# Stick-breaking projections as 512-column blocks that are turned on VectorE and fetched back from device memory

## The chip, the core and the metric
One core of one Trainium2 chip runs the whole program in one launch. The metric is the device time of that launch in microseconds, the median of several runs; here 1634.8 us (three runs, 1633.47 to 1635.04). The rows below come from one profiled execution, which took 1634.64 us and has a span of 1632.9 us from its first to its last instruction.

## The reference
Two decoder layers over 256 tokens with 2048 features, each with a residual sub-layer and a cross-attention sub-layer, and one final RMSNorm. The change lies in the sub-layer of the second (odd) layer, which is stick-breaking attention with 16 heads of 128 features:

```python
u = h @ w_in_odd[o]                     # (256, 2048) @ (2048, 8192)
q, k, v, gate = jnp.split(u, 4, axis=-1)
z = einsum('bhtd,bhsd->bhts', qb, kb) * scale
log_keep = where(mask, log_sigmoid(-z), 0)
rev = cumsum(log_keep[..., ::-1])[..., ::-1] - log_keep
A = where(mask, exp(log_sigmoid(z) + rev), 0)
att = A @ v
x = x + (att * silu(gate)) @ w_out_odd[o]
```

Everything else (pooling mixer and HGRN2 in the first layer, a cross-attention with four heads after each) is unchanged in what it computes.

## The kernel before
All large products run in full precision by splitting each float32 operand into a high part (fp32r) and a low part: a product is hi*hi + hi*lo + lo*hi. The weights come as units of 256 output columns, 136 of them (names `C_KV0` to `C_END` number them), each in four pieces of 512 KB. For every piece, SyncE loads it into `raw`, ScalarE writes its high part into `wpair` (`split_hi`, line 684), VectorE its low part (`split_lo`, line 985), and TensorE multiplies. `wpair` holds exactly one unit, so the split of a piece can begin only when TensorE has done the same piece of the unit before, and has to be finished when TensorE comes round again, three pieces later.

TensorE, ScalarE and VectorE each have an order written out by hand. `slot(c, steps)` is what ScalarE or VectorE does while TensorE is in unit c: for p in 0 to 3, split piece p of unit c+1, then the steps listed at p. A step marked `END` stands ahead of the split at p = 3 and waits for the end of unit c. On TensorE, a hook `(p, work)` runs behind piece p. All engines work strictly in this order, so a step that waits holds up all splits behind it.

There are two forms of product. `chunk(..., "T")` (lines 345, 348) keeps the weights still and moves the tokens: one unit, 256 features on the partitions by 256 tokens, per k-tile two matmuls of 512 columns and two of 256. `block` (line 393) keeps the tokens still and moves 512 weight columns: two units at once, tokens on the partitions, per k-tile six matmuls of 512 columns. What comes out of a block stands the other way round. Where features are needed on the partitions, `turn_block` transposes 32 by 32 squares on VectorE, SyncE stores the 512 KB into a small tensor in device memory (`key_store`, line 243) and fetches them back with the squares in their places, in four DMAs (line 248). The two residual stages and the cross-attention keys already do this.

The stick-breaking stage (`C_SB`, units 80 to 111) goes pair by pair of heads, i = 0 to 7. Values of eight heads at a time come as two blocks; queries, keys and gate of each pair are three chunks. For a pair, TensorE computes the logits z (`sb_logits`, lines 634, 636), ScalarE and VectorE make softplus (900 to 906, 1443, 1447), VectorE its reversed running sum (1456, 1461), ScalarE the exponential (913), VectorE masks it (1469, `sb_weights`); then TensorE turns the weights (`turn`, line 645), ScalarE copies them (926), TensorE multiplies them with the values (`mix_values`, 653, 655), and `sb_outputs` (1484 to 1489) applies the gate. Turning and mixing of pair i are hooks in the first unit of pair i+1; the last pair's are hooks of the output stage `out_stage(C_OUT1)`.

In an `out_stage` the residual is brought up to date unit by unit, and GpSimd scales and squares each unit (lines 1569, 1553, 1555), while ScalarE (711) and VectorE (1181) split the scaled unit into high and low parts. In the stage `C_OX0`, VectorE also splits the features of the memory (`mem1_lo`, line 1020) for the stage behind it, `C_KV1`.

## Time and profile before

| what | value |
|---|---|
| median of three runs | 1634.8 us |
| the profiled execution | 1634.64 us, span 1632.9 us |
| TensorE busy | 1622.3 us, 99% of the span |
| VectorE busy | 1139.3 us, 70% |
| ScalarE busy | 792.3 us, 49% |
| GpSimd busy | 150.7 us, 9% |
| stick-breaking stage | 949.7 to 1330.3 us of the span |

The busy time of TensorE says that it nearly always has a matmul in flight, and not how fast it goes: neighbouring matmuls overlap, so the distance between their starts is what a unit costs. VectorE and ScalarE have time to spare on average, but within one pair of heads their steps form a chain that TensorE waits for at its end.

### The profile page before, as it was taken

The numbers are of one execution on the slowest core, as the hardware profiler recorded it, in microseconds if no ns is written. First come the engines' busy times: TensorE is split into PE (matmuls) and PEld (weight loads), VectorE is DVE, ScalarE is ACT, GpSimd is POOL, SyncE is SP. The second block draws the span as 40 slices with busy tenths as digits, with TensorE's granted clock in tenths as the row PEclk, the third lists the DMA queues.
The fourth block names the chain that finished last, engine by engine and source line by source line (L and its number), as shares of the span: only waits on it lengthen the run. The fifth ranks groups of instructions, "written<-read, shape, count | busy, mean of one in ns | idle before, by whom it ended". The sixth has DMA issues, their size and how long they took to land.

```text
span 1632.9 us, 22719 instructions
## 1 busy us (share of the span) xinstructions
PE 1622.3 (99%) x8842; PEld 1393.6 (85%) x8842; DVE 1139.3 (70%) x1273; ACT 792.3 (49%) x957; POOL 150.7 (9%) x103
## 2 busy tenths in 40 slices
...
GB/s 283 243 250 195 217 193 168 168 181 156 167 179 203 221 170 141 154 202 241 224 242 226 193 192 185 179 168 168 185 177 162 187 175 220 198 168 160 149 188 135
DMA packets 243236, 310.61 MB, mean 190 GB/s; under 512 B 10192, under 2 KB 181584, under 8 KB 243024
## 3 DMA queue, kind: packets, MB, share of 16 engines
...
## 4 chain that ended last, share of the span: by engine, by line
PE 96%; DVE 1%; DMA 1%; ACT 1%; SPq 0%; issue 0%; ACTq 0%
PE ps L345 35%; PE ps L393 32%; PE ps L348 17%; PE ps L410 5%; PE ps L489 1%; PE ps L469 1%; DMA raw<-xa_wkv 1%; PE ps L645 0%; PE ps L636 0%; PE ps L653 0%; PE ps L549 0%; DVE wpair L985 0%; SPq L283 0%; PE ps L572 0%; PE ps L480 0%; DVE ypair L1020 0%
## 5 line engine op out<-in xcount | busy, mean ns | idle before, releaser
L985 DVE TENSOR_TENSOR wpair<-raw,wpair 128x1024 fp32r<-128x1024 f32 x536 | 692.0, 1300 | 377.0 <-ACT wpair L684 375.1
L684 ACT ACTIVATE wpair<-raw 128x1024 fp32r<-128x1024 f32 x536 | 567.7, 1060 | 731.0 <-PE ps L348 389.5
L345 PE MATMUL ps<-xpair,wpair 128*128 128x512 f32 x1920 | 608.3, 398 | 0.0
L393 PE MATMUL ps<-wpair,ypair 128*128 128x512 f32 x1920 | 440.1, 391 | 1.9 <-DVE ypair L1020 1.9
L348 PEld LDWEIGHTS ps<-xpair,wpair 128*128 128x128 f32 x1920 | 360.7, 188 | 85.1
L393 PEld LDWEIGHTS ps<-wpair,ypair 128*128 128x128 f32 x1920 | 360.6, 188 | 76.9 <-issue 2.2
L348 PE MATMUL ps<-xpair,wpair 128*128 128x256 f32 x1920 | 377.5, 278 | 0.0
L345 PEld LDWEIGHTS ps<-xpair,wpair 128*128 128x128 f32 x1920 | 293.7, 189 | 2.0 <-issue 0.6
L345 PE MATMUL ps<-ypair,wpair 128*128 128x512 f32 x448 | 140.9, 396 | 0.0
L1569 POOL TENSOR_TENSOR scratch<-xT,par 128x512 f32<-128x512 f32 x24 | 29.4, 1223 | 824.2 <-issue 771.6
L348 PEld LDWEIGHTS ps<-ypair,wpair 128*128 128x128 f32 x448 | 84.2, 188 | 19.9
L1004 DVE TENSOR_REDUCE tmp<-ps 128x512 f32<-128x1024 f32 x66 | 80.6, 1220 | 21.8 <-PE ps L348 21.7
L410 PE MATMUL ps<-wpair,ypair 128*128 128x512 f32 x384 | 88.5, 390 | 0.0
L348 PE MATMUL ps<-ypair,wpair 128*128 128x256 f32 x448 | 88.0, 278 | 0.0
L393 PE MATMUL ps<-wpair,xpair 128*128 128x512 f32 x384 | 87.9, 390 | 0.0
L393 PEld LDWEIGHTS ps<-wpair,xpair 128*128 128x128 f32 x384 | 71.9, 188 | 14.8
L410 PEld LDWEIGHTS ps<-wpair,ypair 128*128 128x128 f32 x384 | 71.6, 188 | 14.7
L345 PEld LDWEIGHTS ps<-ypair,wpair 128*128 128x128 f32 x448 | 68.4, 189 | 0.4 <-DVE tmp L1230 0.2
L1555 POOL TENSOR_TENSOR acc<-acc,sq 128x512 f32<-128x512 f32 x24 | 42.1, 1755 | 1.9
L345 PE MATMUL ps<-wpair,xpair 128*128 128x512 f32 x128 | 40.5, 397 | 0.0
L1553 POOL TENSOR_TENSOR sq<-xT 128x512 f32<-128x512 f32 x24 | 38.9, 1619 | 0.0
L348 PEld LDWEIGHTS ps<-wpair,xpair 128*128 128x128 f32 x128 | 24.0, 188 | 5.7
...
## 6 DMA issues: line engine op xcount, KB each, us to landing
raw<-w_in_odd SPq DMA_DIRECT2D x128, 512.0 KB, 3.9
...
```

The costliest lines, as they stand in the source:

```text
L345: mm(ps[:, 2 * parity + j, :], still[:, k, 0, j * P:(j + 1) * P], move[:, k].rearrange("p h n -> p (h n)"), start=(k == 0), stop=False)
L348: last = mm(ps[:, 2 * parity + j, S:2 * S], still[:, k, 1, j * P:(j + 1) * P], move[:, k, 0], start=False, stop=(k == KT - 1))
L393: last = mm(ps[:, 2 * parity + r, :].rearrange("p (b n) -> p b n", b=2), operand[:, k, x_part, r * P:(r + 1) * P], wpair[:, KP * p + 2 * a ...
L410: last = mm(ps[:, 2 * (e % 2) + r, :].rearrange("p (b n) -> p b n", b=2), ypair[:, k, x_part, r * P:(r + 1) * P], wpair[:, KP * p + 2 * a: ...
L469: last = mm(ps[:, 4, r * S:(r + 1) * S].rearrange("p (m a t) -> p m a t", m=2, a=4), xq_qp[:, k, q_part, r * P:(r + 1) * P], in_rows(ypair ...
L489: last = mm(ps[:, 6 + b // 2, (b % 2) * S:(b % 2 + 1) * S], xq_v[:, m, v_part, b * P:(b + 1) * P], xq_pt[:, m, p_part, :], start=(m == 0 a ...
L684: fn(wpair[:, KP * p:KP * (p + 1), 0, :], raw[:, p], ACT.Copy).then_inc(hi_ready, 1)
L985: v.tensor_tensor(wpair[:, kp, 1, :], raw[:, p], wpair[:, kp, 0, :].bitcast(F32), ALU.subtract).then_inc(lo_ready, 1)
L1004: v.tensor_reduce(dst, ps[:, 2 * parity:2 * parity + 2, :].rearrange("p j (h n) -> p j n h", h=2), AX.X, ALU.add).then_inc(evac_done, 1)
L1553: g.tensor_tensor(sq[:], block_ap, block_ap, ALU.mult).then_inc(s["x_sq"], 1)
L1555: ins = g.tensor_tensor(acc[:], acc[:], sq[:], ALU.add)
L1569: g.tensor_tensor(out_xg, xT[:, blk, :], gb, ALU.mult).then_inc(s["xg_ready"], 1)
```

## The change
In the stick-breaking stage, queries, keys and gates of the first twelve heads come as blocks too, two units each for four heads, in the order query, key, value, gate, for n = 0, 1, 2. Query, key and gate blocks are turned on VectorE, stored to device memory, fetched into a landing area of 1024 columns and multiplied by the row of reciprocal norms on VectorE (`sb_take_turned`, four multiplications of 128x256 each). The last four heads have a value block and a query block, and their keys and gates stay chunks. Fourteen blocks and four chunks stand where four blocks and twenty-four chunks stood. The steps of a pair are spread over other slots. In `out_stage`, the ScalarE and VectorE steps of residual units 2, 3, 5 and 6 each stand one or more pieces earlier. The four semaphores of the last outputs become two, and `final_gain` is loaded behind `sb_y` instead of `sb_tr`. The diff, cut to its core:

```diff
-        sb_q, sb_k, sb_v, sb_sg = view(0, 2, S), view(512, 2, S), view(5888, 2, 1024), view(1536, 2, S)
-        sb_l, sb_sp, sb_a = view(2048, 2, 3 * P), view(2816, 2, 3 * P), view(3584, 2, 3 * P)
-        sb_rc, sb_at = view(4352, 2, 3 * P), view(5120, 2, 3 * P)
+        sb_q, sb_k, sb_v, sb_g = view(0, 4, S), view(1024, 4, S), view(2048, 2, 512), view(3072, 4, S)
+        sb_land, sb_sg = scratch[:, 4096:4096 + 4 * S], view(3072, 2, S)
+        sb_l, sb_sp, sb_a, sb_at = (view(5120 + 768 * j, 2, 3 * P) for j in range(4))
+        sb_rc = sb_l
+        sb_row = mrs[:, 0:S]
+        tmp_flat = tmp.rearrange("p a b n -> p (a b) n")
...
+        SB_LAST = C_SB + 24
+        SB_TURNED = [(8 * n + 2 * j, 11 + 3 * n + i) for n in range(3) for i, j in enumerate((0, 1, 3))] + [(26, 20)]
...
-            for i in range(8):
-                if i % 4 == 0:
-                    wide(C_SB + 4 * i, W_ino, 2 * D + i * CH, range(2))
-                for j, base in enumerate((0, D, 3 * D)):
-                    load_chunk(sb_chunk(i, j), W_ino, base + i * CH)
-            out_stage(C_OUT1, W_outo, 11)
+            def sb_after(at):
+                for first, n in SB_TURNED:
+                    if at == (first + 3) * 4 + 3:
+                        store(n)
+                    if at == (first + 4) * 4 + 1:
+                        if n > 11:
+                            taken, count = (("sb_gate", 0), ("sb_qr", 1), ("sb_kr", 1))[(n - 11) % 3]
+                            sp.wait_ge(s[taken], (n - 11) // 3 + count)
+                        fetch(n, sb_land)
+
+            for n in range(3):
+                for j, base in enumerate((0, D, 2 * D, 3 * D)):
+                    wide(C_SB + 8 * n + 2 * j, W_ino, base + n * 512, range(1), first=C_SB, after=sb_after)
+            for j, base in enumerate((2 * D, 0)):
+                wide(SB_LAST + 2 * j, W_ino, base + 3 * 512, range(1), first=C_SB, after=sb_after)
+            for j, col in enumerate((D + 6 * CH, 3 * D + 6 * CH, D + 7 * CH, 3 * D + 7 * CH)):
+                for p in range(NP):
+                    load_piece(SB_LAST + 4 + j, p, W_ino, col)
+                    sb_after((28 + j) * 4 + p)
+            out_stage(C_OUT1, W_outo, 21)
...
+                    pe.wait_ge(s["sb_qr"], i // 2 + 1)
+                    pe.wait_ge(s["sb_kr"], i // 2 + 1 if i < 6 else i - 2)
...
-            for i in range(8):
-                tail = sb_tail(i - 1, 2, 3) if i else ()
-                if i % 4 == 0:
-                    c = C_SB + 4 * i
-                    block(c, 0, xpair, c + 1 if i else c, hooks=tail)
-                    block(c + 2, 1, xpair, c + 2)
-                    tail = ()
-                chunk(sb_chunk(i, 0), sb_parity(i, 0), xpair, "T", hooks=tail, evacuated=0 if i % 4 == 0 else 1)
-                chunk(sb_chunk(i, 1), sb_parity(i, 1), xpair, "T")
-                chunk(sb_chunk(i, 2), sb_parity(i, 2), xpair, "T", hooks=((1, sb_logits(i)),))
+            for n in range(3):
+                c, a = C_SB + 8 * n, 2 * n
+                block(c, 0, xpair, c, hooks=sb_tail(a - 1, 2, 3) if n else ())
+                block(c + 2, 1, xpair, c + 2)
+                block(c + 4, 0, xpair, c + 4, hooks=((7, sb_logits(a)),))
+                block(c + 6, 1, xpair, c + 6, hooks=sb_tail(a, 4, 5) + ((5, sb_logits(a + 1)),))
+            block(SB_LAST, 0, xpair, SB_LAST, hooks=sb_tail(5, 2, 3))
+            block(SB_LAST + 2, 1, xpair, SB_LAST + 2)
+            chunk(SB_LAST + 4, 0, xpair, "T", evacuated=0)
+            chunk(SB_LAST + 5, 1, xpair, "T", hooks=((2, sb_logits(6)),))
+            chunk(SB_LAST + 6, 0, xpair, "T", hooks=sb_tail(6, 2, 3))
+            chunk(SB_LAST + 7, 1, xpair, "T", hooks=((1, sb_logits(7)),))
...
-                slot(c0 + 6, ((1, hi(2)), (3, hi(3))))
-                slot(c0 + 7, ((0, hi(5)), (2, hi(6))) + after + (() if after else ((3, hi(7)),)))
+                slot(c0 + 6, ((0, hi(2)), (1, hi(3)), (3, hi(5))))
+                slot(c0 + 7, ((1, hi(6)),) + after + (() if after else ((3, hi(7)),)))
...
+            for n in range(3):
+                c, a = C_SB + 8 * n, 2 * n
+                slot(c, ((0, sb_weights(a - 1)), (2, sb_turned(a - 1))) if n else ())
+                slot(c + 1, ((2, sb_sigmoid(n - 1)), (3, sb_hi(a - 2))) if n else ())
+                slot(c + 2, ((0, sb_hi(a - 1)),) if n else ())
+                slot(c + 3)
+                slot(c + 4)
+                slot(c + 5, ((3, sb_softplus(a)),))
+                slot(c + 6, ((2, sb_weights(a)),))
+                slot(c + 7, ((0, sb_turned(a)), (1, sb_softplus(a + 1))))
+            slot(SB_LAST, ((0, sb_weights(5)), (2, sb_turned(5))))
+            slot(SB_LAST + 1, ((2, sb_sigmoid(2)), (3, sb_hi(4))))
+            slot(SB_LAST + 2, ((0, sb_hi(5)),))
+            slot(SB_LAST + 3)
+            slot(SB_LAST + 4)
+            slot(SB_LAST + 5, ((2, sb_softplus(6)),))
+            slot(SB_LAST + 6, ((1, sb_weights(6)), (1, sb_sigmoid(3)), (2, sb_turned(6))))
+            slot(SB_LAST + 7, ((0, sb_hi(6)), (1, sb_softplus(7))))
+            out_stage(C_OUT1, 2, ((0, sb_weights(7)), (0, sb_sigmoid(4)), (2, sb_turned(7)), (3, sb_hi(7))))
...
-                slot(c0 + 6, ((1, lo(2)), (3, lo(3)), (END, add_product(6))))
+                slot(c0 + 6, ((0, lo(2)), (1, lo(3)), (3, lo(5)), (END, add_product(6))))
                 last = ((3, add_product(7)),) if after else ((END, add_product(7)), (3, lo(7)))
-                slot(c0 + 7, ((0, lo(5)), (2, lo(6))) + after + last)
+                slot(c0 + 7, ((1, lo(6)),) + after + last)
...
+            def sb_take_turned(n, dst, done, row=rs_row):
+                def work():
+                    dve.wait_ge(s["keys_in"], 64 * n)
+                    r_row = row.rearrange("p (r a t) -> p a r t", r=2, a=4)
+                    for k in range(4):
+                        part = sb_land.rearrange("p (a k r t) -> p k a r t", a=4, k=4, r=2)[:, k]
+                        out_k = dst[:, k, :].rearrange("p (r a t) -> p a r t", r=2, a=4)
+                        last = v.tensor_tensor(out_k, part, r_row, ALU.mult)
+                    last.then_inc(s[done], 1)
+                return work
...
-            for i in range(8):
-                tail = ((0, sb_weights(i - 1)), (3, sb_outputs(i - 1))) if i else ()
-                if i % 4 == 0:
-                    c = C_SB + 4 * i
-                    slot(c, tail)
-                    slot(c + 1, ((END, sb_values(c, 0, i)),))
-                    slot(c + 2)
-                    slot(c + 3, ((END, sb_values(c + 2, 1, i)),))
-                    tail = ()
-                slot(sb_chunk(i, 0), ((END, sb_queries(i)),) + tail)
-                slot(sb_chunk(i, 1), ((END, sb_keys(i)),))
-                slot(sb_chunk(i, 2), ((1, sb_softplus(i)), (2, sb_cumulate(i)), (END, sb_gate(i))))
-
-            out_stage(C_OUT1, 2, 11, ((0, sb_weights(7)), (3, sb_outputs(7))))
+            for n in range(3):
+                c, a = C_SB + 8 * n, 2 * n
+                slot(c, ((0, sb_weights(a - 1)),) if n else ((0, sb_query_row),))
+                slot(c + 1, ((END, turn_block(c, 0, 11 + 3 * n)),) +
+                     (((1, sb_gates(n - 1)), (3, sb_outputs(a - 2))) if n else ()))
+                slot(c + 2, ((0, sb_outputs(a - 1)),) if n else ())
+                slot(c + 3, ((2, sb_take_turned(11 + 3 * n, sb_q, "sb_qr", sb_row)), (END, turn_block(c + 2, 1, 12 + 3 * n))))
+                slot(c + 4)
+                slot(c + 5, ((1, sb_take_turned(12 + 3 * n, sb_k, "sb_kr")), (END, sb_values(c + 4, n))))
+                slot(c + 6, ((0, sb_softplus(a)), (1, sb_cumulate(a)), (2, sb_weights(a))))
+                slot(c + 7, ((2, sb_softplus(a + 1)), (3, sb_cumulate(a + 1)), (END, turn_block(c + 6, 1, 13 + 3 * n))))
+            slot(SB_LAST, ((0, sb_weights(5)),))
+            slot(SB_LAST + 1, ((1, sb_gates(2)), (END, sb_values(SB_LAST, 3)), (3, sb_outputs(4))))
+            slot(SB_LAST + 2, ((0, sb_outputs(5)),))
+            slot(SB_LAST + 3, ((END, turn_block(SB_LAST + 2, 1, 20)),))
+            slot(SB_LAST + 4, ((END, sb_keys(6)),))
+            slot(SB_LAST + 5, ((1, sb_take_turned(20, sb_q, "sb_qr", sb_row)), (3, sb_softplus(6)), (END, sb_gate(6))))
+            slot(SB_LAST + 6, ((0, sb_cumulate(6)), (1, sb_weights(6)), (END, sb_keys(7))))
+            slot(SB_LAST + 7, ((0, sb_outputs(6)), (2, sb_softplus(7)), (3, sb_cumulate(7)), (END, sb_gate(7))))
+
+            out_stage(C_OUT1, 2, 21, ((0, sb_weights(7)), (3, sb_outputs(7))))
```

VectorE, before: the last pair (i = 7), from its softplus on. `wpair<-raw,wpair` is the split of a piece, `sb_ln` comes from ScalarE's softplus, line 1004 is the evacuation of the gate unit.

```order
L985 TENSOR_TENSOR wpair<-raw,wpair 128x4x256 [waits hi_ready] x3
L1443 SCALAR_TENSOR_TENSOR scratch<-ps,scratch 128x384 [waits sb_ln] x2
L1447 TENSOR_TENSOR scratch<-scratch,cst 128x384 [waits sb_sp0] x2
L985 TENSOR_TENSOR wpair<-raw,wpair 128x4x256 [waits hi_ready]
L1456 SCALAR_TENSOR_TENSOR scratch<-cst,scratch 128x128 [waits sb_sp1]
L1456 SCALAR_TENSOR_TENSOR scratch<-cst,scratch 128x256
L1456 SCALAR_TENSOR_TENSOR scratch<-cst,scratch 128x128 [waits sb_sp1]
L1456 SCALAR_TENSOR_TENSOR scratch<-cst,scratch 128x256
L1461 TENSOR_TENSOR scratch<-ps,scratch 128x384 [waits sb_cum] x2
L1004 TENSOR_REDUCE tmp<-ps 128x512 [waits piece_done]
L1477 TENSOR_TENSOR tmp<-tmp,rs 128x512 [waits evac_done]
L985 TENSOR_TENSOR wpair<-raw,wpair 128x4x256 [waits hi_ready] x2
```

The weights (line 1469) follow directly. VectorE, now: the last pair again. Lines 1539 to 1544 are the outputs of pair 6, 1495 and 1499 the softplus of pair 7, 1037 and 1531 its gate, 1508 the running sum.

```order
L1539 TENSOR_TENSOR tmp<-tmp,scratch 128x512 [waits sb_gsig]
L1542 TENSOR_TENSOR tmp<-ps,tmp 128x512 [waits sb_av,sb_gg]
L1544 TENSOR_TENSOR ypair<-tmp,ypair 128x2x256 [waits y_hi]
L1018 TENSOR_TENSOR wpair<-raw,wpair 128x4x256 [waits hi_ready] x2
L1495 SCALAR_TENSOR_TENSOR scratch<-ps,scratch 128x384 [waits sb_ln] x2
L1499 TENSOR_TENSOR scratch<-scratch,cst 128x384 [waits sb_sp0] x2
L1037 TENSOR_REDUCE tmp<-ps 128x512 [waits piece_done,ypair_ready]
L1531 TENSOR_TENSOR tmp<-tmp,rs 128x512 [waits evac_done]
L1018 TENSOR_TENSOR wpair<-raw,wpair 128x4x256 [waits hi_ready]
L1508 SCALAR_TENSOR_TENSOR scratch<-cst,scratch 128x128 [waits sb_sp1]
```

The outputs of the pair before have moved in directly ahead of this pair's softplus, the gate's evacuation stands between softplus and running sum, and behind the running sum one split is left ahead of the weights instead of evacuation and two splits.

VectorE, now: pair 6, the first one of the last four heads, from the evacuation of its keys to its softplus. Line 1465 is the multiplication of the fetched queries, 1488 the end of the keys.

```order
L1037 TENSOR_REDUCE tmp<-ps 128x512 [waits piece_done,sb_gg]
L1488 TENSOR_TENSOR scratch<-tmp,rs 128x512 [waits evac_done]
L1018 TENSOR_TENSOR wpair<-raw,wpair 128x4x256 [waits hi_ready] x3
L1465 TENSOR_TENSOR scratch<-scratch,mrs 128x4x2x32 [waits keys_in]
L1465 TENSOR_TENSOR scratch<-scratch,mrs 128x4x2x32 x3
L1018 TENSOR_TENSOR wpair<-raw,wpair 128x4x256 [waits hi_ready]
L1037 TENSOR_REDUCE tmp<-ps 128x512 [waits piece_done]
L1531 TENSOR_TENSOR tmp<-tmp,rs 128x512 [waits evac_done]
L1018 TENSOR_TENSOR wpair<-raw,wpair 128x4x256 [waits hi_ready]
L1495 SCALAR_TENSOR_TENSOR scratch<-ps,scratch 128x384 [waits sb_ln] x2
```

The queries are finished behind the split at p = 1 of unit `SB_LAST + 5`, and TensorE's logits of pair 6 are a hook behind piece 2 of that unit. The softplus stands behind the gate's evacuation, which waits for the end of the unit.

VectorE, now: the second pair of a group of four heads (i = 1, 3, 5), softplus to weights. Line 1184 is the turning of the gate block.

```order
L1495 SCALAR_TENSOR_TENSOR scratch<-ps,scratch 128x384 [waits sb_ln] x2
L1499 TENSOR_TENSOR scratch<-scratch,cst 128x384 [waits sb_sp0] x2
L1184 STREAM_TRANSPOSE turned<-ps 128x4x4x32 [waits keys_in,piece_done]
L1184 STREAM_TRANSPOSE turned<-ps 128x4x4x32
L1018 TENSOR_TENSOR wpair<-raw,wpair 128x4x256 [waits evac_done,hi_ready]
L1508 SCALAR_TENSOR_TENSOR scratch<-cst,scratch 128x128 [waits sb_sp1]
L1508 SCALAR_TENSOR_TENSOR scratch<-cst,scratch 128x256
L1508 SCALAR_TENSOR_TENSOR scratch<-cst,scratch 128x128 [waits sb_sp1]
L1508 SCALAR_TENSOR_TENSOR scratch<-cst,scratch 128x256
L1513 TENSOR_TENSOR scratch<-ps,scratch 128x384 [waits sb_cum] x2
L1018 TENSOR_TENSOR wpair<-raw,wpair 128x4x256 [waits hi_ready]
L1521 SCALAR_TENSOR_TENSOR scratch<-scratch,cst 128x384 [waits sb_aexp] x2
```

Where before the gate's evacuation stood behind the running sum, the turning of a block stands ahead of it.

## Rows read from the trace of the kernel before

**Rows 1.** The page: span, busy time by engine, the chain that ended last
```profile
span 1632.9 us, 22719 instructions
PE 1622.3 (99%) x8842; PEld 1393.6 (85%) x8842; DVE 1139.3 (70%) x1273; ACT 792.3 (49%) x957; POOL 150.7 (9%) x103
...
PE 96%; DVE 1%; DMA 1%; ACT 1%; SPq 0%; issue 0%; ACTq 0%
```

**Rows 2.** Windows: two chunk units, then two block units (us, busy by engine, granted clock)
```profile
993.24:1015.53 22.29, 22.29 (x130) 19.46 (x129) 13.04 (x12) 8.49 (x8) 0.00 (x0) 1.00 0.63 192
949.72:971.48 21.76, 21.76 (x98) 18.02 (x96) 11.12 (x10) 8.48 (x8) 0.00 (x0) 1.00 0.66 192
```

**Rows 3.** Timeline of VectorE, pair 0, softplus to weights (start, duration, instruction, idle before)
```profile
1025.86 1.02 DVE L1443 SCALAR_TENSOR_TENSOR scratch<-ps,scratch 128x384 f32<-128x384 f32 x2 [2.19 <-ACT scratch L906]
...
1027.74 1.22 DVE L985 TENSOR_TENSOR wpair<-raw,wpair 128x1024 fp32r<-128x1024 f32 x1
1028.88 1.90 DVE L1456 TENSOR_TENSOR_SCAN scratch<-cst,scratch 128x128 f32<-128x128 f32 x4
1030.69 0.99 DVE L1461 TENSOR_TENSOR scratch<-ps,scratch 128x384 f32<-128x384 f32 x2
1031.60 1.21 DVE L1004 TENSOR_REDUCE tmp<-ps 128x512 f32<-128x1024 f32 x1
...
1033.46 2.35 DVE L985 TENSOR_TENSOR wpair<-raw,wpair 128x1024 fp32r<-128x1024 f32 x2
1035.73 1.02 DVE L1469 SCALAR_TENSOR_TENSOR scratch<-scratch,cst 128x384 f32<-128x384 f32 x2
```

**Rows 4.** Timeline of TensorE: the logits of pair 0 and the turning of its weights
```profile
1021.10 0.38 PE L634 MATMUL ps<-scratch 128*128 128x128 f32 x2
...
1036.34 1.01 PE L645 MATMUL ps<-cst,scratch 128*128 128x128 f32 x6
```

**Rows 5.** Timeline of ScalarE: split, table load and softplus of pair 0
```profile
1021.35 1.06 ACT L684 ACTIVATE wpair<-raw 128x1024 fp32r<-128x1024 f32 x1 [1.73 <-PE ps L348]
1022.43 1.28 ACT L897 ACT_TABLE_LOAD   x1
...
1026.14 1.05 ACT L684 ACTIVATE wpair<-raw 128x1024 fp32r<-128x1024 f32 x1
```

**Rows 6.** Timeline of VectorE: outputs of pair 0, and ScalarE's part in them
```profile
1043.18 0.68 DVE L1484 TENSOR_TENSOR tmp<-tmp,scratch 128x512 f32<-128x512 f32 x1
```
```profile
1044.62 0.63 ACT L930 ACTIVATE ypair<-tmp 128x512 fp32r<-128x512 f32 x1 [3.33 <-DVE tmp L1487]
```

**Rows 7.** Timeline of VectorE in `C_OUT1`: four multiplications of fetched data, turning of a block
```profile
1375.90 1.43 DVE L1164 TENSOR_TENSOR xT<-scratch,xT 128x256 f32<-128x256 f32 x4
1377.25 1.30 DVE L1151 STREAM_TRANSPOSE turned<-ps 128x512 f32<-128x512 f32 x2
1378.70 4.11 DVE L985 TENSOR_TENSOR wpair<-raw,wpair 128x1024 fp32r<-128x1024 f32 x2
```

**Rows 8.** Timeline of SyncE in `C_OUT1`: store and fetch; landing times of all fetches
```profile
1357.70 0.51 SPq L243 DMA_DIRECT2D key_store<-turned  x1
...
1363.31 1.76 SPq L248 DMA_DIRECT2D scratch<-key_store  x4
```
```profile
DMA to landing us min/median/max: 2.9/4.3/6.2
```

**Rows 9.** End of `C_OX0`: VectorE, GpSimd, TensorE, and a window of the clock behind it
```profile
768.61 4.25 DVE L1020 SCALAR_TENSOR_TENSOR ypair<-xkT,par,ypair 128x256 fp32r<-128x256 f32 x4
...
773.91 1.66 DVE L1020 SCALAR_TENSOR_TENSOR ypair<-xkT,par,ypair 128x256 fp32r<-128x256 f32 x4
```
```profile
768.85 1.12 POOL L1569 TENSOR_TENSOR scratch<-xT,par 128x512 f32<-128x512 f32 x1 [0.72 <-DVE xpair L1181]
```
```profile
773.00 17.31 PE L393 MATMUL ps<-wpair,ypair 128*128 128x512 f32 x68 [1.87 <-DVE ypair L1020]
```
```profile
773.00:778.00 5.00, 5.00 (x15) 3.95 (x16) 5.00 (x9) 3.08 (x7) 0.00 (x0) 0.66 0.38 114
```

More of the change, by code:

```diff
@@ L185, in build @@
             xa_q xa_qhi xa_qlo xa_khi xa_klo xa_vhi xa_vlo xa_ptlo xa_scores xa_max xa_exp xa_rs xa_p xa_ptr xa_pt xa_pv xa_hi
-            sb_qr sb_kr sb_z sb_abs sb_exp sb_ln sb_sp0 sb_sp1 sb_cum sb_log sb_tr sb_at sb_aexp sb_am sb_vr sb_av sb_gate sb_gsig sb_gg sb_y
+            sb_row sb_qr sb_kr sb_z sb_abs sb_exp sb_ln sb_sp0 sb_sp1 sb_cum sb_log sb_tr sb_at sb_aexp sb_am sb_vr sb_av sb_gate sb_gsig sb_gg sb_y
             cs_zero row_done fin_gain fin_sq fin_part fin_mean fin_root fin_rs""".split()
         s = {n: sem(n) for n in names}
-        fin_out = [[sem(f"fin_out{half}{r}") for r in range(2)] for half in range(2)]
+        fin_out = [sem(f"fin_out{half}") for half in range(2)]
         def head_slot(g, j):
@@ L926, in turned, with sb_hi, work @@
                         fn(sb_at[:, h, :], ps[:, 4 + h, 0:3 * P], ACT.Copy).then_inc(s["sb_at"], 1)
-                def output_hi():
+                return work
+            def sb_hi(i):
+                def work():
                     act.wait_ge(s["sb_y"], i + 1)
-                    fn(ypair[:, 2 * i:2 * i + 2, 0, :], tmp[:, sb_parity(i, 2)], ACT.Copy).then_inc(s["y_hi"], 1)
-                return ((0, sb_weights(i)), (0, sb_sigmoid(i)), (turn_at, turned), (hi_at, output_hi))
-            for i in range(8):
-                tail = sb_tail(i - 1, 2, 3) if i else ()
-                if i % 4 == 0:
-                    for t in range(4):
-                        slot(C_SB + 4 * i + t, tail if t == 0 else ())
-                    tail = ()
-                slot(sb_chunk(i, 0), tail)
-                slot(sb_chunk(i, 1))
-                slot(sb_chunk(i, 2), ((1, sb_softplus(i)),))
-            out_stage(C_OUT1, 2, sb_tail(7, 2, 3))
+                    src = sb_g[:, i % 2 * 2:i % 2 * 2 + 2, :] if i < 6 else tmp[:, 1]
+                    fn(ypair[:, 2 * i:2 * i + 2, 0, :], src, ACT.Copy).then_inc(s["y_hi"], 1)
+                return work
+            for n in range(3):
[17 more added lines that the diff above has]
+            out_stage(C_OUT1, 2, ((0, sb_weights(7)), (0, sb_sigmoid(4)), (2, sb_turned(7)), (3, sb_hi(7))))
             act.wait_ge(s["keys_in"], 10 * 64)
```

96 lines of the change are left out of this document (52 added, 44 removed).

## The prediction
> **What bounds the kernel now.** The page comes first: TensorE is busy for 99% of the span and makes 96% of the chain that ended last [rows 1]. So only two things can move the time: how fast TensorE gets through a unit of 256 weight columns, and whether it waits. The windows answer the first: two chunk units take 22.29 us and two units as one block 21.76 us [rows 2], though both send the same number of columns through the array. That is 11.145 against 10.88 us a unit, a piece (a quarter) 2.79 against 2.72 us. The timelines answer the second. TensorE starts the logits of pair 0 at 1021.10 and the turning of its weights at 1036.34 [rows 4]; VectorE starts these weights at 1035.73, and the first of the two is finished half of 1.02 us later, at 1036.3 [rows 3]. The chain from logits to weights is thus exactly as long as TensorE's way to the turning: five chunk pieces and 1.3 us for the logits, 15.2 us. Nothing is in reserve there. This decides the case: each edit that lengthens the chain, or shortens TensorE's way, makes TensorE wait.
>
> **Blocks for chunks.** 28 units of the stage are block units where 8 were, so 20 units get 0.265 us cheaper: -5.3 us. Logits, turning and mixing keep their matmuls and cost the same. The weights are the same bytes.
>
> A rule of the Trainium skill speaks against this gain. TensorE: Matmul & The Clock Gate (Wait — 56ns, not 53.3ns?) gives a matmul N columns at 2.4 GHz plus 2.5 ns, 215.7 ns for 512 and by the same formula 109.2 ns for 256. By it a block unit (48 matmuls) would cost 10.35 us and a chunk unit (32 and 32) 10.40 us, and the edit would save 0.9 us instead of 5.3. The windows disagree, so their numbers stand in the sum.
>
> **The yardsticks of the chain.** On VectorE, from one start to the next [rows 3]: softplus 1.88 us (1025.86 to 1027.74), a split 1.14, the running sum with its subtraction 2.72 (1028.88 to 1031.60), evacuating and scaling a chunk 1.86 (1031.60 to 1033.46), the first weight 0.55. ScalarE starts its split 0.25 us after TensorE starts the next piece and needs 1.06; table load and softplus hold its next split back by 3.7 us (1022.43 to 1026.14) [rows 5]. VectorE's split follows ScalarE's, so it begins 1.3 us after the end of a piece and is over, for what follows, at 2.45.
>
> **First pair of four heads (three times).** Counted from the logits: ScalarE's split behind softplus runs from 5.0 to 6.1, then on VectorE split, softplus, split, sum, split and first weight: 6.1 + 1.14 + 1.88 + 1.14 + 2.72 + 1.14 + 0.55 = 14.7. TensorE is there at 1.3 + 5 x 2.72 = 14.9. No wait.
>
> **Second pair (three times).** Counted from the end of the piece behind the logits: split done at 2.45, softplus 4.3, turning the gate block 1.45 [rows 7], split, sum, split, weight: 2.45 + 1.88 + 1.45 + 1.14 + 2.72 + 1.14 + 0.55 = 11.3. TensorE is there after four pieces, 10.9. A wait of 0.5 us with the semaphore, 1.5 us in all.
>
> **Queries of pair 6 (once).** They are multiplied behind the split at p = 1: 2.45 + 1.35 for four multiplications [rows 7] + 0.1 = 3.9 after the end of that piece. TensorE's logits are due one piece on, at 2.8. Wait 1.1 us.
>
> **Weights of pair 6 (once).** Only four pieces lie between its logits and its turning, where five lay before. From the end of the unit with the gate: 0.2, evacuation 1.86, split, softplus, split, sum, split, weight = 10.65. TensorE is due after three pieces, 8.35. Wait 2.3 us.
>
> **Weights of pair 7 (once).** From the end of piece 0 of the last unit: split 2.45; the outputs of pair 6 give ScalarE its copy 1.44 us later, at 3.9, and its next split starts 0.55 us on [rows 6], ends at 5.5; table and softplus 3.7, 9.2; split, 10.3. Then VectorE: 10.3 + 1.14 + 1.88 + 1.86 + 1.14 + 2.72 + 1.14 + 0.55 = 20.7. TensorE has one chunk piece, the logits, two chunk pieces and three block pieces to go: 17.8. Wait 2.9 us. Of the five steps this is the largest, and it falls into the output stage.
>
> **The clock behind a wait.** At the end of C_OX0 TensorE stands idle for 1.87 us and starts at 773.00 [rows 9]. In the 5 us behind that, the granted clock is 0.66 in the mean: for a stretch it fell from the 2.4 GHz level to the 1.2 GHz one and came back. A third of 5 us is 1.7 us lost on top of the wait. The waits of 2.3 and 2.9 us are longer than that one, so I charge 1.7 us to each, 3.4 us. No row shows what a wait of 1.1 or 0.5 us does; I take nothing for these, and 1.7 us for the 1.1 as the upper bound.
>
> **Store and fetch.** Ten blocks go out and come back. In C_OUT1 the fetch follows the store by 5.6 us and is issued in 1.8; the longest landing of any was 6.2 us [rows 8]: at most 13.6 us from the store. A turned block is used at p = 1 of the second unit on: 10.9 + 5.4 + 2.45 = 18.8 us after the end of its last unit. The gate block's store stands behind half a softplus, turning, split and issue, some 4.9 us after that end, so its use comes 13.9 us behind the store. The keys have 14.5 us, and a piece's slack before their logits. So I cost them at nothing; the cover is thin. VectorE's own load does not grow: three multiplied takes and three turnings stand for six evacuations with scaling. The longest heap of steps, two outputs with a turning ahead of them, leaves its splits some 2 us ahead of TensorE.
>
> **Residual units.** In C_OX0 two residual splits leave the pieces at the end. There VectorE's four feature splits take 4.25 us while GpSimd works, and 1.66 us a piece later when it rests [rows 9]; they are what TensorE waits for. In the new order I follow the units: unit 5 is done some 1.5 us sooner on VectorE, but this starts GpSimd on unit 6 at nearly the time at which it started before (768.85), so the feature splits meet it again. I take 0.4 us off the wait and leave the clock's fall as it is: -0.4. The bounds are 0 and -3.6 (the wait of 1.87 and its 1.7).
>
> GPSIMD Engine Reference (1. Specifications) of the Trainium skill says that GpSimd shares its SBUF interfaces with VectorE and contends with instructions with two SBUF inputs. The feature splits are such, and the trace agrees with its 4.25 against 1.66 us. The multiplications of fetched data are too, but GpSimd has no work in the stick-breaking stage, so the rule adds nothing there.
>
> **Sum.** -5.3 + 1.5 + 1.1 + 2.3 + 2.9 + 3.4 - 0.4 = +5.5 us on the profiled execution's 1634.6, which lies within 0.2 us of the median: 1640.2 us.
>
> **Rivals.**
> - The clock falls behind one of the two long waits only, or behind neither: 1638.5 or 1636.8. For it: one observation is all there is. Against: both waits are longer than the one observed.
> - The C_OX0 wait vanishes with its clock loss: 1640.2 - 3.2 = 1637.0. It decides whether GpSimd's unit 6 is over when the features begin; 3 us of shift would do it, and my shift is 1.5.
> - Other side: the hooks find their weights ready, as pair 0 does before, because a step of the chain is sooner than I read it. Faster than 1631.5 needs all waits together under some 2.5 us and so no fallen clock: 1634.6 - 5.3 + 1.5 - 0.4 = 1630.4, and 1627 if C_OX0 clears too. Against it: the order on VectorE is fixed, and the gate's evacuation ahead of the softplus of pair 6 waits for the end of its unit whatever else is fast.
> - The fetches land later than 14 us behind the store. VectorE then holds the splits; above about 2 us TensorE waits, up to three times: 1643 to 1646.
> - Chunk and block cost the same here after all, by the page's rule above: 1640.2 + 4.4 = 1644.6.
>
> **Chances.** Forecast 0.36; clock falls once 0.14 (of this 0.10 above the bound of slower); neither falls 0.07; C_OX0 clears 0.15; hooks ready 0.18; late fetches 0.08; no gain of blocks 0.02. A difference under 0.2% (3.3 us) can't be told from none: slower 0.56, same 0.26, faster 0.18. The forecast's own range is 1638 to 1642.5. From 1633 to 1643 the range leaves out the faster case and the last two in part.
>
> **What would show it.** Windows of the new stage: 21.76 us per block everywhere. TensorE's waits at the turning of pair 7 (3 us), pair 6 (2), at the logits of pair 6 (1), at the turning of pairs 1, 3 and 5 (0.5 each) and none at 0, 2 and 4, all on VectorE. A granted clock near 0.66 for 5 us behind the first two. At C_KV1 a wait of 1.5 us, VectorE again. The prediction is wrong if the turning of pair 7 starts without a wait, if the clock stays full behind it, if a take of fetched data waits for its DMA, or if C_KV1 starts on time.

## The result and the profile after

The changed kernel takes 1636.87 us in the median (1635.16 to 1642.57, 18 runs). On the same chip the kernel before takes 1634.20 us (1633.20 to 1635.19, 18 runs). The ratio is 1.0022, with a 95% interval of 1.0016 to 1.0029: slower by 2.7 us in the median. The ratio is one of means (1637.74 against 1634.15 us), and the interval leaves out 1: a small loss, but clear of the noise. The profiled execution took 1638.71 us.

The page of the changed kernel, against [rows 1]:

```profile
span 1636.8 us, 22179 instructions
PE 1620.3 (99%) x8522; PEld 1381.9 (84%) x8522; DVE 1130.4 (69%) x1294; ACT 787.2 (48%) x951; POOL 153.6 (9%) x103
PE 93%; DVE 5%; ACT 1%; issue 0%; DMA 0%; POOL 0%; ACTq 0%; DVEq 0%; POOLq 0%
```

VectorE has 5% of the chain that ended last, and TensorE less than the 96% of before. So TensorE now waits for VectorE. What TensorE waited for (line, releaser: us in total, times, longest):

```profile
PE ps L660 <- DVE scratch L1521: 6.1, 5, 2.8
PE ps L522 <- DVE sq L1230: 1.1, 1, 1.1
PE ps L650 <- DVE scratch L1465: 1.0, 1, 1.0
PE ps L534 <- DVE wpair L1252: 0.9, 1, 0.9
PE ps L407 <- DVE ypair L1053: 0.8, 1, 0.8
```

L660 is the turning of the weights, L650 the logits; L522 and L534 are the start-up, which both kernels have. TensorE's timeline places the new waits (start, duration, instruction, idle before), at the turning of pairs 4, 5, 6 and 7 and, third, the logits of pair 6:

```profile
1217.59 0.82 PE L660 MATMUL ps<-cst,scratch 128*128 128x128 f32 x6
1237.77 1.01 PE L660 MATMUL ps<-cst,scratch 128*128 128x128 f32 x6 [0.38 <-DVE scratch L1521]
1296.06 0.49 PE L650 MATMUL ps<-scratch 128*128 128x128 f32 x2 [1.02 <-DVE scratch L1465]
1310.93 1.54 PE L660 MATMUL ps<-cst,scratch 128*128 128x128 f32 x6 [2.15 <-DVE scratch L1521]
1340.86 1.25 PE L660 MATMUL ps<-cst,scratch 128*128 128x128 f32 x6 [2.80 <-DVE scratch L1521]
```

Pairs 1 and 3 wait 0.39 and 0.38 us like pair 5. The windows (the third value from the end is the granted clock) show a stretch of blocks at the pace of [rows 2] (97 matmuls in 21.76 us, 98 there), the stretches behind the waits of 2.15 and 2.80 us, and the one behind the start of `C_KV1` that [rows 9] has at 0.66:

```profile
1065.00:1086.76 21.76, 21.76 (x97) 18.02 (x97) 14.33 (x16) 9.91 (x12) 0.00 (x0) 1.00 0.79 224
1311.00:1316.00 5.00, 5.00 (x23) 4.49 (x24) 1.57 (x2) 2.46 (x5) 0.00 (x0) 0.68 0.44 135
1342.00:1346.00 4.00, 4.00 (x13) 3.15 (x13) 2.36 (x2) 2.35 (x4) 0.00 (x0) 0.64 0.51 151
773.00:778.00 5.00, 5.00 (x23) 4.11 (x22) 5.00 (x10) 4.59 (x9) 0.00 (x0) 1.00 0.37 108
```

Behind both long waits the clock falls to the 1.2 GHz level and comes back. Behind `C_KV1` it stays at 2.4 GHz. There TensorE now waits 0.82 us instead of 1.87:

```profile
765.45 1.80 DVE L1214 TENSOR_TENSOR xpair<-scratch,xpair 128x512 fp32r<-128x512 f32 x1
767.17 1.21 DVE L1018 TENSOR_TENSOR wpair<-raw,wpair 128x1024 fp32r<-128x1024 f32 x1
768.30 4.28 DVE L1053 SCALAR_TENSOR_TENSOR ypair<-xkT,par,ypair 128x256 fp32r<-128x256 f32 x4
...
```
```profile
767.42 1.86 POOL L1631 TENSOR_TENSOR scratch<-xT,par 128x512 f32<-128x512 f32 x1 [0.72 <-DVE xpair L1214]
```

The four features still meet GpSimd's unit 6 and still take 4.3 us. But they begin at 768.30, 0.3 us sooner than before, while TensorE is due at 771.9 (its start less its wait), 0.8 us later than the 771.1 of before. So against TensorE the features begin 1.1 us sooner, but TensorE starts `C_KV1` at 772.73 instead of 773.00, only 0.27 us sooner. Where the 0.8 us come from is seen in the first experiment.

### The profile page after: what moved, and what is told of

Its sections match the earlier page's. It is cut to its first block, busy times and chain, and to the rows that moved or that the text cites. A ratio compares the mean times of both kernels' runs of the same rounds, so it can differ in the third digit from the quotient of the medians.

```text
span 1636.8 us, 22179 instructions
## 1 busy us (share of the span) xinstructions
PE 1620.3 (99%) x8522; PEld 1381.9 (84%) x8522; DVE 1130.4 (69%) x1294; ACT 787.2 (48%) x951; POOL 153.6 (9%) x103
## 4 chain that ended last, share of the span: by engine, by line
PE 93%; DVE 5%; ACT 1%; issue 0%; DMA 0%; POOL 0%; ACTq 0%; DVEq 0%; POOLq 0%
PE ps L407 43%; PE ps L359 25%; PE ps L362 12%; PE ps L424 5%; DVE wpair L1018 2%; PE ps L503 1%; PE ps L483 1%; PE ps L534 1%; ACT wpair L701 1%; DVE scratch L1508 1%; PE ps L537 0%; PE ps L660 0%; PE ps L669 0%; PE ps L563 0%; PE ps L651 0%
## 5 line engine op out<-in xcount | busy, mean ns | idle before, releaser
L359 PE MATMUL ps<-xpair,wpair 128*128 128x512 f32 x1280 | 406.6, 399 | 0.0
L407 PE MATMUL ps<-wpair,xpair 128*128 128x512 f32 x1344 | 309.6, 391 | 0.0
L407 PEld LDWEIGHTS ps<-wpair,xpair 128*128 128x128 f32 x1344 | 251.7, 188 | 51.9
L362 PEld LDWEIGHTS ps<-xpair,wpair 128*128 128x128 f32 x1280 | 241.0, 188 | 56.6
L362 PE MATMUL ps<-xpair,wpair 128*128 128x256 f32 x1280 | 252.3, 279 | 0.0
L359 PEld LDWEIGHTS ps<-xpair,wpair 128*128 128x128 f32 x1280 | 196.3, 189 | 1.6 <-issue 0.6
L1631 POOL TENSOR_TENSOR scratch<-xT,par 128x512 f32<-128x512 f32 x24 | 35.1, 1462 | 826.6 <-issue 777.0
L1037 DVE TENSOR_REDUCE tmp<-ps 128x512 f32<-128x1024 f32 x46 | 56.2, 1221 | 15.9 <-PE ps L362 15.8
L359 PE MATMUL ps<-wpair,xpair 128*128 128x512 f32 x128 | 40.5, 398 | 0.0
L1615 POOL TENSOR_TENSOR sq<-xT 128x512 f32<-128x512 f32 x24 | 33.9, 1414 | 0.0
L1214 DVE TENSOR_TENSOR xpair<-scratch,xpair 128x512 fp32r<-128x512 f32 x24 | 26.4, 1098 | 8.0 <-ACT xpair L728 8.0
```

Source lines behind the costliest of these rows:

```text
L359: mm(ps[:, 2 * parity + j, :], still[:, k, 0, j * P:(j + 1) * P], move[:, k].rearrange("p h n -> p (h n)"), start=(k == 0), stop=False)
L362: last = mm(ps[:, 2 * parity + j, S:2 * S], still[:, k, 1, j * P:(j + 1) * P], move[:, k, 0], start=False, stop=(k == KT - 1))
L407: last = mm(ps[:, 2 * parity + r, :].rearrange("p (b n) -> p b n", b=2), operand[:, k, x_part, r * P:(r + 1) * P], wpair[:, KP * p + 2 * a ...
L1037: v.tensor_reduce(dst, ps[:, 2 * parity:2 * parity + 2, :].rearrange("p j (h n) -> p j n h", h=2), AX.X, ALU.add).then_inc(evac_done, 1)
L1214: v.tensor_tensor(xpair[:, 2 * u:2 * u + 2, 1, :], out_xg, xpair[:, 2 * u:2 * u + 2, 0, :].bitcast(F32), ALU.subtract).then_inc(xpair_read ...
L1615: g.tensor_tensor(sq[:], block_ap, block_ap, ALU.mult).then_inc(s["x_sq"], 1)
```

## The experiments

All run beside the kernel before, which took 1634.17 us in the first four and 1634.38 us in the last four.

**The residual units alone.** The kernel before with this edit, on ScalarE and the same on VectorE (cut):

```diff
-slot(c0 + 6, ((1, hi(2)), (3, hi(3))))
-slot(c0 + 7, ((0, hi(5)), (2, hi(6))) + after + ...
+slot(c0 + 6, ((0, hi(2)), (1, hi(3)), (3, hi(5))))
+slot(c0 + 7, ((1, hi(6)),) + after + ...
```

> The kernel before with only the residual units moved, as in the changed kernel. Theory: the forecast undersized this part. In the changed kernel's profile TensorE waits 0.82 us at C_KV1 where it waited 1.87 us before, and the clock stays at 1.00 behind it where it was 0.66 over 5 us, so this edit alone gives back 1.05 + 1.7 = 2.7 us: 1634.2 - 2.7 = 1631.5 us. Rival: the forecast's own term, 0.4 us: the wait is about 1.5 us, the clock falls as before, 1633.8 us, and then the full clock in the changed kernel's profile was chance.

Measured: 1632.54 us (11 runs), ratio 0.9991 (0.9982 to 1.0000). TensorE's wait and the window behind it:

```profile
PE ps L393 <- DVE ypair L1020: 0.8, 1, 0.8
773.00:778.00 5.00, 5.00 (x23) 4.10 (x23) 5.00 (x10) 4.68 (x9) 0.00 (x0) 1.00 0.35 108
```

Wait and clock are as the theory says, but the median gains 1.6 us, not 2.7. The timelines show two reasons, and the single times a third.

A fall of the clock at `C_KV1` costs 1.1 us there and not 1.7. From the start of `C_KV1` to the next sum of squares (`L365`) TensorE takes 20.77 us in the kernel before (773.00 to 793.77), where the clock fell, and 19.66 us in this one (772.75 to 792.41), where it didn't. At the full clock TensorE's weight loads wait for VectorE's splits in this stretch (the idle time stands in the row of the weight loads, PEld); in the kernel before they have no such wait, so 0.8 us of the fall is hidden:

```profile
783.88 5.31 PEld L393 LDWEIGHTS ps<-wpair,ypair 128*128 128x128 f32 x24 [0.40 <-DVE wpair L985]
789.55 2.60 PEld L393 LDWEIGHTS ps<-wpair,ypair 128*128 128x128 f32 x12 [0.36 <-DVE wpair L985]
```

And TensorE is 0.8 us late long before `C_KV1`. Its first products, in the kernel before and then in this one:

```profile
6.54 0.70 PE L520 MATMUL ps<-ypair,wpair 128*128 128x512 f32 x2 [0.85 <-DVE wpair L1219]
7.32 0.62 PE L520 MATMUL ps<-ypair,wpair 128*128 128x512 f32 x2
```
```profile
6.59 1.19 PE L520 MATMUL ps<-ypair,wpair 128*128 128x512 f32 x2 [0.89 <-DVE wpair L1219]
8.00 1.05 PE L520 MATMUL ps<-ypair,wpair 128*128 128x512 f32 x2
```

The same four matmuls take 0.78 us there and 1.41 here, and the slow pace lasts to about 10.4 us, although the granted clock reads 1.00 in windows there. The first `L365` starts at 38.28 and at 39.07 us, and the 0.8 us stay up to `C_OX0`. Ahead of `C_OUT0` the two kernels have the same code. The slow start is in all five profiled executions with the moved residual units and in none of the five without; yet the profiled execution of this kernel is also the slowest of its 11, 0.8 us above their median, which would fit a slow start that comes by chance. Whether the edit causes it stays open. In these two executions TensorE starts `C_KV1` only 0.25 us sooner; with the 1.1 us of clock that makes the 1.3 us between their spans (1632.9 and 1631.6).

The third reason is chance. The 16 runs of the kernel before fall into those with a mean clock of 0.999, at 1632.77 to 1633.93 us (7), and those with 0.998, at 1634.11 to 1635.40 us (9): in some executions the clock doesn't fall behind its wait of 1.87 us. The trace of the kernel with waits made to measure (below), which has the same code up to there, shows one: the same wait of 1.87 us, and behind it

```profile
773.00:778.00 5.00, 5.00 (x24) 4.12 (x23) 5.00 (x10) 3.08 (x6) 0.00 (x0) 1.00 0.46 129
```

All 11 runs of the kernel with the moved units lie within 1.3 us (1632.06 to 1633.34). Its wait isn't always 0.8 us, though: the profiled execution of the second-pairs version below waits 1.55 us at `C_KV1`, with the same order there, and without a fall.

**The residual units put back in the changed kernel** (the same edit the other way).

> The changed kernel with the residual units put back where they were. Theory: it loses the 2.7 us again: 1636.9 + 2.7 = 1639.6 us, with a wait of 1.9 us at C_KV1 and a granted clock near 0.66 behind it. Rival (the term was 0.4): 1637.3 us.

Measured: 1639.42 us (1637.25 to 1640.59, 6 runs), ratio 1.0034 (1.0022 to 1.0046), the median that the theory has. The profiled execution is the fastest of the six, and shows what chance does. The windows behind `C_KV1` and behind the turning of pairs 6 and 7:

```profile
PE ps L407 <- DVE ypair L1053: 2.0, 1, 2.0
773.00:778.00 5.00, 5.00 (x24) 4.11 (x23) 5.00 (x10) 3.71 (x7) 0.00 (x0) 1.00 0.45 129
1311.00:1316.00 5.00, 5.00 (x31) 4.38 (x32) 2.73 (x3) 3.47 (x6) 0.00 (x0) 1.00 0.45 139
1342.00:1346.00 4.00, 4.00 (x16) 3.30 (x16) 1.65 (x3) 1.98 (x4) 0.00 (x0) 0.70 0.52 164
```

The waits were 2.02, 2.15 and 2.80 us, and the clock fell behind the last one only. TensorE starts `C_KV1` at 772.65 here and at 772.73 in the changed kernel, which had the slow start; so the longer wait alone doesn't account for the 2.5 us between the medians. The mean clocks point to more falls: 0.998 at most in the six runs, 0.999 in 7 of the 18 of the changed kernel.

**The last section respaced.** The changed kernel with its query block first, and with the hooks of pairs 6 and 7 where the kernel before had them (cut; ScalarE's steps and the store move with them):

```diff
 TensorE
-chunk(SB_LAST + 5, 1, xpair, "T", hooks=((2, sb_logits(6)),))
+chunk(SB_LAST + 5, 1, xpair, "T", hooks=((1, sb_logits(6)),))
 VectorE
-slot(SB_LAST + 5, ((1, sb_take_turned(20, ...)), (3, sb_softplus(6)), (END, sb_gate(6))))
-slot(SB_LAST + 6, ((0, sb_cumulate(6)), (1, sb_weights(6)), (END, sb_keys(7))))
-slot(SB_LAST + 7, ((0, sb_outputs(6)), (2, sb_softplus(7)), (3, sb_cumulate(7)), (END, sb_gate(7))))
+slot(SB_LAST + 3, ((2, sb_take_turned(20, ...)), (END, sb_values(SB_LAST + 2, 3, 2))))
+slot(SB_LAST + 5, ((1, sb_softplus(6)), (2, sb_cumulate(6)), (END, sb_gate(6))))
+slot(SB_LAST + 6, ((0, sb_weights(6)), (END, sb_keys(7)), (3, sb_outputs(6))))
+slot(SB_LAST + 7, ((1, sb_softplus(7)), (2, sb_cumulate(7)), (END, sb_gate(7))))
```

> The changed kernel with the last section of the stick-breaking stage spaced as the kernel before had it: its query block comes first, the logits stand five pieces ahead of the turning, softplus and running sum at p = 1 and 2. Theory: the waits of 1.02, 2.15 and 2.80 us go, and with the two long ones the 1.7 us of fallen clock behind each: 1636.9 - 6.0 - 3.4 = 1627.5 us. Rival A: in most executions the clock does not fall behind these waits and only they go: 1630.9 us. Rival B: VectorE is so full there that its splits come late instead, and TensorE waits for these: 1633 us or more, with waits on wpair in the last eight units.

Measured: 1628.48 us (1628.12 to 1629.35, 5 runs), ratio 0.9964 (0.9951 to 0.9978). The three waits are gone and none took their place:

```profile
PE ps L660 <- DVE scratch L1521: 1.2, 3, 0.4
```

That is 8.4 us less than the changed kernel: 6.0 us of waits, and 2.4 us that are left for the clock. It lies nearer to the theory (3.4) than to rival A (none). In the profiled execution of the changed kernel the two falls cost 1.4 and 1.6 us: from the turning of pairs 6 and 7 to their mixing (`L669`) TensorE takes 5.02 and 5.21 us, here 3.64 and 3.63. The moves were made together, so what each of them gives wasn't tried.

**Waits made to measure.** The kernel before, with idle work ahead of the first weight of each pair:

```diff
+DELAY = (0, 4, 8, 12, 16, 20, 24, 32)
 for h in range(2):
     dve.wait_ge(s["sb_aexp"], i * 2 + (h + 1))
+    if h == 0 and DELAY[i]:
+        v.tensor_reduce(sb_sp[:, 0, 0:DELAY[i]], ones.unsqueeze(1).to_broadcast([P, DELAY[i], P]),
+                        AX.X, ALU.add)
```

> The kernel before with a reduction of 0.5 to 4.3 us on VectorE ahead of the first weight of pairs 1 to 7 (4, 8, 12, 16, 20, 24 and 32 rows of 128 columns, estimated 0.133 us each); nothing reads what it writes. Theory: nothing is in reserve on that chain, so TensorE waits 0.5, 1.1, 1.6, 2.1, 2.7, 3.2 and 4.3 us, 15.5 in all, and the clock falls to 0.5 for some 3.4 us behind those from 2.1 us up and not behind those up to 1.1 us: 4 falls of 1.7 us, 1634.2 + 15.5 + 6.8 = 1656.5 us, 1658 if the 1.6 us wait has one too. Rival A: the falls in the two profiles had other causes than the length of the wait: 1649.7 us. Rival B: the chain has a reserve of about 1 us that the profile hides: the first two waits are absent and all others 1 us shorter, 1650 us with four falls.

Measured: 1656.13 us (1655.78 to 1656.77, 4 runs), ratio 1.0136 (1.0120 to 1.0151). TensorE's timeline at the turning of pairs 3, 4, 5 and 7, and the windows behind each of them:

```profile
1148.98 1.01 PE L645 MATMUL ps<-cst,scratch 128*128 128x128 f32 x6 [1.68 <-DVE scratch L1474]
1231.88 1.01 PE L645 MATMUL ps<-cst,scratch 128*128 128x128 f32 x6 [2.03 <-DVE scratch L1474]
1273.09 1.22 PE L645 MATMUL ps<-cst,scratch 128*128 128x128 f32 x6 [2.56 <-DVE scratch L1474]
1357.48 1.54 PE L645 MATMUL ps<-cst,scratch 128*128 128x128 f32 x6 [4.35 <-DVE scratch L1474]
```
```profile
1149.00:1154.00 5.00, 5.00 (x27) 4.24 (x28) 2.73 (x4) 2.01 (x3) 0.00 (x0) 1.00 0.71 229
1232.00:1237.00 5.00, 5.00 (x22) 4.17 (x23) 2.56 (x3) 0.95 (x2) 0.00 (x0) 0.66 0.54 179
1273.00:1278.00 5.00, 4.91 (x20) 4.18 (x21) 2.78 (x4) 0.98 (x2) 0.00 (x0) 0.66 0.46 140
1357.00:1362.00 5.00, 4.52 (x14) 3.85 (x15) 3.16 (x4) 0.98 (x2) 0.00 (x0) 0.50 0.35 97
```

The seven waits (0.43, 0.96, 1.68, 2.03, 2.56, 3.10 and 4.35 us) sum to 15.1 us and the median is 22.0 us above the kernel before; the other 6.9 us are four falls. From turning to mixing TensorE takes 3.61 to 3.65 us behind the three shortest waits and 5.21, 5.21, 5.04 and 5.81 us behind the others: 1.6, 1.6, 1.4 and 2.2 us more, 6.8 in all. Behind 4.35 us the clock had fallen some 1.8 us before the wait ended, and yet this fall cost the most. Rival A and rival B are out. The first wait, 0.43 us after a delay of 0.5, shows that the chain has next to nothing in reserve.

**Seven waits of one length.** The same with `DELAY = (0, 14, 14, 14, 14, 14, 14, 14)`:

> The kernel before with the same reduction (14 rows) ahead of the first weight of each of pairs 1 to 7: seven waits of about 1.85 us, 13 us in all. Theory: at this length the fall of the clock is a matter of chance, as with the 1.87 us wait of the kernel before, whose times fall into two groups 1.5 us apart: some 4 of 7 falls on average, 1634.2 + 13 + 6.8 = 1654 us, spread from run to run in steps of 1.7 us. Rival A: only the length decides, and every wait has its fall or none has: 1659 or 1647 us, with no spread.

Measured: 1653.16 us (4 runs: 1650.63, 1652.13, 1654.19, 1655.14), ratio 1.0111. The waits sum to 12.7 us by the profile's view, and to 13.4 by the way from logits to turning, which takes 17.16 us each time instead of 15.24; so 5.3 us, or 3.4 falls of 1.6, are left in the median. In the profiled execution four of seven equal waits have a fall, those at pairs 1, 3, 5 and 6. The waits of pairs 1, 2 and 3, the start of the mixing of pairs 1 and 2, and the windows:

```profile
1075.90 1.02 PE L645 MATMUL ps<-cst,scratch 128*128 128x128 f32 x6 [1.76 <-DVE scratch L1474]
...
1081.10 0.59 PE L653 MATMUL ps<-scratch 128*128 128x256 f32 x2
...
1116.30 1.01 PE L645 MATMUL ps<-cst,scratch 128*128 128x128 f32 x6 [1.76 <-DVE scratch L1474]
1119.94 0.60 PE L653 MATMUL ps<-scratch 128*128 128x256 f32 x2
...
1155.15 1.07 PE L645 MATMUL ps<-cst,scratch 128*128 128x128 f32 x6 [1.95 <-DVE scratch L1474]
```
```profile
1076.00:1082.00 6.00, 6.00 (x28) 5.10 (x29) 3.29 (x4) 1.61 (x3) 0.00 (x0) 0.72 0.68 224
1116.00:1122.00 6.00, 5.70 (x35) 5.00 (x36) 4.81 (x6) 2.02 (x3) 0.00 (x0) 1.00 0.70 231
1155.00:1161.00 6.00, 5.85 (x23) 4.71 (x24) 2.83 (x4) 1.38 (x3) 0.00 (x0) 0.72 0.71 240
```

Two waits of exactly 1.76 us went different ways: 5.20 us from turning to mixing behind the first, 3.64 behind the second. At this length the wait doesn't decide the outcome.

**The same with 10 rows**, `DELAY = (0, 10, 10, 10, 10, 10, 10, 10)`:

> As the last with 10 rows: seven waits of about 1.3 us, 9.2 us in all. Theory: a wait this short has no fall: 1634.2 + 9.2 = 1643.4 us. Rival: the chance of a fall goes down with the length but is not nil at 1.3 us: about one or two falls, 1645 to 1647 us.

Measured: 1643.61 us (1642.39 to 1644.21, 5 runs), ratio 1.0055 (1.0042 to 1.0069). The waits (1.22 to 1.42 us) sum to 9.0, and 1634.38 + 9.0 = 1643.4. From turning to mixing it is 3.60 to 3.64 us in all seven: no fall behind a wait this short.

**The second pair of each four heads one piece earlier**, on top of the respaced last section:

```diff
-slot(c + 7, ((2, sb_softplus(a + 1)), (3, sb_cumulate(a + 1)), (END, turn_block(...))))
+slot(c + 7, ((1, sb_softplus(a + 1)), (2, sb_cumulate(a + 1)), (END, turn_block(...))))
```

> The kernel with the last section respaced, and besides the softplus and the running sum of the second pair of each four heads one piece earlier on VectorE (p = 1 and 2 in place of 2 and 3). Theory: the three waits of 0.39 us at the turning of pairs 1, 3 and 5 go and nothing takes their place: 1628.5 - 1.2 = 1627.3 us. Against the kernel before, with the residual units worth 1.6 to 2.5 us, that leaves 4.4 to 5.3 us for the blocks in place of chunks (5.3 forecast, 0.9 by the page's rule, which would give 1631 us). Rival: the sum, now ahead of a split, makes that split late, and TensorE waits for wpair: 1628.5 us or more.

Measured: 1626.41 us (1625.75 to 1627.72, 5 runs), ratio 0.9951 (0.9937 to 0.9964). This is the fastest version of all, 8.0 us under the kernel before. Against the kernel with only the last section respaced it gains 2.1 us and not 1.2. TensorE's timeline for pair 1 with the section respaced only, and then with this edit (logits, turning, mixing):

```profile
1033.26 0.39 PE L650 MATMUL ps<-scratch 128*128 128x128 f32 x2
...
1048.73 1.01 PE L660 MATMUL ps<-cst,scratch 128*128 128x128 f32 x6 [0.39 <-DVE scratch L1521]
1052.77 0.38 PE L670 MATMUL ps<-scratch 128*128 128x128 f32 x2
```
```profile
1033.92 0.39 PE L650 MATMUL ps<-scratch 128*128 128x128 f32 x2
...
1048.85 0.82 PE L660 MATMUL ps<-cst,scratch 128*128 128x128 f32 x6
1052.68 0.38 PE L670 MATMUL ps<-scratch 128*128 128x128 f32 x2
```

From logits to turning it is 15.47 us with the wait and 14.93 without, 0.54 us where the view of waits has 0.39; from turning to mixing (`L670`) 4.04 and 3.83. That is 0.75 us a pair, 2.25 for the three. Of the part inside the turning the view of waits has 0.16 us, in the row of weight loads and not in TensorE's: it is the wait for the second head's weight.

**Features ahead of residual unit 5**, on top of the last. ScalarE, and the same on VectorE:

```diff
-slot(c0 + 6, ((0, hi(2)), (1, hi(3)), (3, hi(5))))
-slot(c0 + 7, ((1, hi(6)),) + after + ...
+slot(c0 + 6, ((0, hi(2)), (1, hi(3))) + ...
+slot(c0 + 7, after[:1] + (((0, hi(5)), (2, hi(6))) + after[1:] ...
```

> As the last, and in C_OX0 the first features of the next stage stand ahead of residual unit 5 on ScalarE and VectorE, units 5 and 6 behind them. Theory: GpSimd rests while VectorE computes these features, they take 1.7 us in place of 4.3, and TensorE's last wait of 0.82 us at C_KV1 goes: 1627.3 - 0.8 = 1626.5 us. Rival: GpSimd's later units delay the sum of squares for the normalization that TensorE takes in C_KV1, and the wait comes back there: 1627.3 us or more.

Measured: 1627.40 us (1626.94 to 1627.55, 5 runs), ratio 0.9958 (0.9944 to 0.9972), 1.0 us above the last and not 0.8 below it. VectorE and TensorE:

```profile
767.47 1.66 DVE L1053 SCALAR_TENSOR_TENSOR ypair<-xkT,par,ypair 128x256 fp32r<-128x256 f32 x4
...
770.79 4.28 DVE L1053 SCALAR_TENSOR_TENSOR ypair<-xkT,par,ypair 128x256 fp32r<-128x256 f32 x4
```
```profile
783.62 8.71 PE L407 MATMUL ps<-wpair,ypair 128*128 128x512 f32 x36 [1.02 <-DVE wpair L1018]
```

The first features take 1.66 us with GpSimd at rest, and `C_KV1` starts without a wait. But now the second four meet GpSimd's unit 6 and take 4.28. VectorE is a split behind 11 us later, where TensorE waits 1.02 us. The rival was right that the wait comes back, and wrong on what would be late.

## Why the prediction was right, and where its sizes were off

Forecast 1640.2 us, measured 1636.87; slower, inside the range of 1633 to 1643, below the forecast's own range (1638 to 1642.5). The mechanism was right: cheaper blocks, and TensorE waiting for VectorE at the hooks that were named. Too large was what it charged for the clock, too small what it gave the residual units, and both put the forecast too high.

- **Blocks for chunks, -5.3: right.** From the start of `C_KV1` to the turning of pair 7 the kernel with the residual units alone takes 564.4 us (772.75 to 1337.18) and the fastest version 558.2 (773.31 to 1331.51). Of the 6.2 us between, 1.0 is not the blocks': six pairs lost their wait inside the turning, 4.07 us from the turning [rows 4] to the mixing at 1040.41 against 3.83 (1048.85 to 1052.68), less 0.07 for the cheaper piece: 6 x 0.17. That leaves 5.2. What makes a block cheaper wasn't tried by itself. The rule of the Trainium skill in TensorE: Matmul & The Clock Gate (Wait — 56ns, not 53.3ns?) made it 0.9, and the measurement decides against it.
- **Second pairs, +1.5: right.** The waits are where they were expected, and moving the hooks gave 0.54 us at the start of each of three turnings, 1.6 in all. The 0.2 us inside each turning are no cost of the change, since every pair has them in the kernel before. Pairs 0, 2 and 4 lost them with the change, which the prediction overlooked: -0.5.
- **Queries and weights of pair 6, weights of pair 7, +1.1, +2.3 and +2.9:** measured 1.02, 2.15 and 2.80. The sum of the chain's pitches, taken from one pair in the old order, held to 0.15 us each in a new one.
- **Clock, +3.4: too large.** Read off a window (a third of 5 us), a fall came out at 1.7 us. On TensorE's timeline the two of the profiled execution cost 1.4 and 1.6, and the one of [rows 9] from which the price was taken cost 1.1, because it hid 0.8 us of waits for splits. And a fall is chance: 2.4 us in the median. The 2.80 us wait had its fall in both traces that have it, the 2.15 us wait in one of two.
- **Residual units, -0.4: the step that was most mis-sized.** It measures -1.6 us in the kernel before, and -2.5 in the changed one. I had followed GpSimd's unit 6, found that it still meets the features, and stopped there. That was true, but the features begin 1.1 us sooner against TensorE and the wait falls to 0.8 us, behind which no trace shows a fall of the clock. The prediction kept both the wait (1.5 us) and its fall. The rival "C_OX0 clears" gave 1637.0 and came out closest, by luck: it wanted the wait gone and GpSimd's unit over, and neither was so.
- **Store and fetch, 0: right.** VectorE waits for no transfer between 1000 and 1350 us of the changed kernel.

From one kernel to the next the measured steps close: -1.6 (residual units in the kernel before), -5.2 (blocks), -1.0 (waits inside the turning of six pairs), then, back from the fastest version to the changed one, +2.25 (second pairs) and +8.4 (last section) make +2.8, against +2.7 measured.

Without the residual units the forecast reads +5.9; the kernel with them put back is at +5.2. What of the 0.7 is waits and what clock can't be told at this spread. Nor was it tried why the residual units give 1.6 us in one kernel and 2.5 in the other; a different number of clock falls in the runs of each is a reason that was only argued.
